# One accumulation instead of two for a sample's value tiles in a hybrid decoder step

## What is computed

```python
# group A, 8 heads of 64: forgetting attention over 1024 paged past tokens (8 pages of 128) and the own one
s = q @ kc * SCALE + (c_q - c_k)           # c: running sum of log-forget values
oa = softmax(s) @ vc
# group B, 8 heads of 64: the last 128 keys at strides 1, 4 and 16 and the own one,
# mixed by their softmax denominators
idx = pos - dil[None, :, None] * j         # dil = 1, 4, 16; j = 0..128
ob = sum_over_dil(w * softmax(q @ k[idx]) @ v[idx])
out = concat(oa, ob) @ w_out
```

## Time and profile before

| | |
|---|---|
| median of 3 runs | 2758.29 us (2755.62 to 2760.85) |
| profiled execution, own time | 2759.74 us |
| its span in the profile | 2757.9 us, 43275 instructions |
| mean granted TensorE clock | 0.979 of full speed |
| busy: PE, PEld | 2631.2 us (95%), 2402.2 us (87%) |
| busy: DVE, ACT, POOL | 1161.8 (42%), 543.9 (20%), 1121.1 us (41%) |
| values of samples L1102 | 192 matmul instructions |
| gathers L1083 | 128 matmul instructions |
| sums L1068 | 128 matmul instructions |
| masks L1291 | 16, median 744 ns |

### The profile page before, as it was taken

The page is one execution under the profiler, slowest core; times in us unless marked ns, Lnnn a source line. Parts: engine busy times, 40 slices in busy tenths (PEclk is TensorE's granted clock), DMA queues, the critical chain, the costliest instruction groups (busy, mean ns, idle before and its releaser), DMA issues.

```text
span 2757.9 us, 43275 instructions
## 1 busy us (share of the span) xinstructions
PE 2631.2 (95%) x16553; PEld 2402.2 (87%) x16553; DVE 1161.8 (42%) x2274; ACT 543.9 (20%) x1263; POOL 1121.1 (41%) x726
## 2 busy tenths in 40 slices
PE   5899988989999999999999998998999999999999
PEld 3787765556689999999999996898999999999999
DVE  4763735656615433333333343144453333333333
ACT  3210106555622100000000033312210000000001
POOL 4423214454575444444443345414464444333330
PEclk8999999999999999999999999999999999999999
DMA  4222226656620211111111111111021111111101
GB/s 116 60 76 85 76 64 190 191 185 193 186 79 16 70 47 46 46 46 46 49 49 46 46 38 35 43 32 47 16 62 47 47 49 49 46 46 49 50 31 62
DMA packets 220766, 189.88 MB, mean 69 GB/s; under 512 B 29571, under 2 KB 173443, under 8 KB 220644
## 3 DMA queue, kind: packets, MB, share of 16 engines
q1 hardware_dynamic: 202084, 163.99, 20.4%
q10 hardware_dynamic: 18560, 24.25, 2.5%
HBM read 171.19 MB, written 17.01 MB: 68 GB/s over the span
## 4 chain that ended last, share of the span: by engine, by line
PE 64%; DVE 4%; POOL 1%; ACT 1%; issue 1%; ACTq 0%; POOLq 0%; DVEq 0%
PE ps L489 61%; DVE hs L448 1%; PE ps L521 1%; PE ps L523 1%; PE ps L522 1%; POOL acc_sq L416 1%; ACT ps L1806 1%; DVE Xl L1881 0%; POOL Xl L462 0%; DVE Xl L462 0%; DVE acc_sq L440 0%; PE ps L1781 0%; POOL Wl L378 0%; PE ps L1918 0%; DVE VM_EARLY L1871 0%
## 5 line engine op out<-in xcount | busy, mean ns | idle before, releaser
L489 PE MATMUL ps<-Xh,Wh 128*128 128x256 f32 (+2 forms) x2712 | 875.6, 323 | 15.3 <-DVE Xl L1881 6.5
L489 PE MATMUL ps<-Xl,Wh 128*128 128x256 f32 (+2 forms) x2712 | 869.6, 321 | 0.0
L489 PE MATMUL ps<-Xh,Wl 128*128 128x256 f32 (+2 forms) x2712 | 868.5, 320 | 0.0
L364 POOL TENSOR_TENSOR Wh<-raw,zeros 128x1024 fp32r<-128x1024 f32 x185 | 367.1, 1984 | 1136.0 <-PE ps L489 790.0
L489 PEld LDWEIGHTS ps<-Xh,Wh 128*128 128x128 f32 x2712 | 512.4, 189 | 20.6 <-issue 8.6
L489 PEld LDWEIGHTS ps<-Xl,Wh 128*128 128x128 f32 x2712 | 512.5, 189 | 1.0 <-issue 0.3
L489 PEld LDWEIGHTS ps<-Xh,Wl 128*128 128x128 f32 x2712 | 512.8, 189 | 0.0
L367 POOL TENSOR_TENSOR Wl<-raw,Wh 128x1024 fp32r<-128x1024 f32 x185 | 455.9, 2464 | 14.5
L1597 DVE TENSOR_TENSOR Hl<-hf,Hh 128x392 fp32r<-128x392 f32 (+1 forms) x132 | 181.3, 1373 | 464.7 <-ACT Hh L1525 464.7
L489 PE MATMUL ps<-Hh,Wh 128*128 128x392 f32 (+2 forms) x1056 | 341.5, 323 | 2.4 <-DVE xT L1606 2.3
L489 PE MATMUL ps<-Hl,Wh 128*128 128x392 f32 (+2 forms) x1056 | 338.7, 321 | 0.0
(11 more groups left out here) (201 smaller groups left out, 2530.3 us busy)
## 6 DMA issues: line engine op xcount, KB each, us to landing
raw<-in_w_gate_up SPq DMA_DIRECT2D x88, 512.0 KB, 3.8
raw<-in_w_down SPq DMA_DIRECT2D x44, 512.0 KB, 3.5
kring<-in_cache_a_k SPq DMA_DIRECT2D x64, 256.0 KB, 3.7
ring<-in_cache_a_v SPq DMA_DIRECT2D x64, 256.0 KB, 3.3
raw<-in_w_in_even SPq DMA_DIRECT2D x25, 512.0 KB, 4.2
raw<-in_w_in_c SPq DMA_DIRECT2D x16, 512.0 KB, 3.8
xs<-in_x_prompt SPq DMA_DIRECT2D x8, 512.0 KB, 4.6
q_prompt<-zt ACTq DMA_DIRECT2D x16, 256.0 KB, 2.0
```

The lines of the kernel that those rows point to most:

```text
L364: pool.tensor_tensor(h[:, :], r[:, :], zeros[:, :].to_broadcast([P, 1024]), ALU.add).then_inc(split_high, 1)
L489: ins = nc.tensor.matmul(out, w, x, start=(j == 0), stop=(j == len(pairs) - 1))
```

## The change

The twelve tiles are accumulated in one step at distance 8 (`VALUES_AT`), three groups of four side by side, semaphore `values_ps`. Page heads keep columns 0 to 7 of `Lp`, the dilated heads get columns 8 to 15, so that the exponential is two instructions and bank 7 holds 16 used rows in each 32. The step waits for all eleven ring slots. The sums need one product for each row group instead of two, there is one reciprocal column and one mask over 128 rows, and one gather of four products with two columns of `hmask` that keep page and dilated rows apart. The copy to `oS` is one instruction. The order and the turns in which the sync engine issues the loads stay; only the name of the semaphore changes.

```diff
-        TURN_AT, SPREAD_AT, SUM_AT, PAGES_AT, DILATED_AT = 6, 7, 8, 8, 9
+        TURN_AT, SPREAD_AT, SUM_AT, VALUES_AT = 6, 7, 8, 8
...
-                    positive_wait(sp, page_ps if j < PAGES else dil_ps, it)
+                    positive_wait(sp, values_ps, it)
...
-                    for g in range(2):
-                        for i in range(4):
-                            last = nc.tensor.matmul(ps[i * LW:(i + 1) * LW, 6, 3 * P + g:3 * P + g + 1], Ls[:, g, :], ones[:, 0:1],
-                                                    start=True, stop=True)
-                if sample_at(u, PAGES_AT + 2) is not None:
-
-                    pe.wait_ge(dch, DCH * sample_at(u, PAGES_AT + 2) + 10)
-                    last = gather(sample_at(u, PAGES_AT + 2), 0)
-                if sample_at(u, DILATED_AT + 2) is not None:
-                    pe.wait_ge(osamp, 2 * sample_at(u, DILATED_AT + 2) + 1)
-                    last = gather(sample_at(u, DILATED_AT + 2), 1)
+                    for i in range(4):
+                        last = nc.tensor.matmul(ps[i * LW:(i + 1) * LW, 6, 3 * P:3 * P + 1], Ls[:, :], ones[:, 0:1], start=True, stop=True)
+                if sample_at(u, VALUES_AT + 2) is not None:
+                    last = gather(sample_at(u, VALUES_AT + 2))
...
-                pe.wait_ge(dmask, 2 * it + g + 1)
+                pe.wait_ge(dmask, it + 1)
                 for c in range(4):
-                    last = nc.tensor.matmul(ps[:, 6, 3 * P + 8 + c:3 * P + 9 + c], MV[0:MROWS[g], c * P:(c + 1) * P],
-                                            ones[0:MROWS[g], 0:1],
-                                            start=True, stop=True)
+                    last = nc.tensor.matmul(ps[:, 6, 3 * P + 2 * c:3 * P + 2 * c + 2], MV[:, c * P:(c + 1) * P],
+                                            hmask[:, HEADS:HEADS + 2], start=True, stop=True)
...
                 pe.wait_ge(dp_done, it + 1)
-                for j in tiles:
-                    if ring_slot(j) is not None:
-                        pe.wait_ge(ring_in[ring_slot(j)], 16 * (it + 1))
+                for j in VALUE_ORDER:
+                    pe.wait_ge(ring_in[ring_slot(j)], 16 * (it + 1))
...
-                for n, j in enumerate(tiles):
-                    rows = slice(LW * (n % 4), LW * (n % 4) + LW)
-                    last = nc.tensor.matmul(ps[rows, 7, :], Lp[:, j, :], value_tile(j), start=(n < 4), stop=(n + 4 >= len(tiles)))
-                last.then_inc(done, 1)
+                for j in range(LOG):
+                    rows = slice(LW * (j % 4), LW * (j % 4) + LW)
+                    last = nc.tensor.matmul(ps[rows, 7, :], Lp[:, j, :], value_tile(j), start=(j < 4), stop=(j + 4 >= LOG))
+                last.then_inc(values_ps, 1)
...
-                    act.activation(Lp[:, :, 0:HEADS], Lb[:, :, :], ACT.Exp).then_inc(dp_done, 1)
+                    act.activation(Lp[:, 0:PAGES + 1, 0:HEADS], Lb[:, 0:PAGES + 1, :], ACT.Exp)
+                    act.activation(Lp[:, PAGES + 1:LOG, HEADS:2 * HEADS], Lb[:, PAGES + 1:LOG, :], ACT.Exp).then_inc(dp_done, 1)
...
-                if sample_at(u - 1, PAGES_AT) is not None:
-                    sample_mask(sample_at(u - 1, PAGES_AT), 0, u + 1)
-                if sample_at(u - 1, DILATED_AT) is not None:
-                    sample_mask(sample_at(u - 1, DILATED_AT), 1, u + 1)
+                if sample_at(u - 1, VALUES_AT) is not None:
+                    sample_mask(sample_at(u - 1, VALUES_AT), u + 1)
```

## The result

The changed kernel takes 2780.6 us (median of 5 runs, 2773.5 to 2781.5), the kernel before in the same comparison 2760.9. The ratio is 1.0068, 95% interval 1.005 to 1.0085: slower by 18.8 us by the ratio (the two medians are 19.8 apart). The forecast was 10 us slower, with 2777 as the upper end of its range; the sign was right, the size came out nearly double, above that end. The profiled execution took 2780.6 us, its span is 2778.8.

A forecast was written before the change was run, and what follows sets the result against it. TensorE's fixed instruction order was taken to bound the attention stage (busy 44.4 of 50 us). Savings -21.2, late-tile waits +21.1 and clock +10.4 gave +10.3 us: forecast 2768 us, 8-in-10 range 2752 to 2777.

The forecast's parts named there:

- (a): TensorE's values: joint step takes 2.70 us like the page step, the dilated step goes, saving 7.9 us.
- (b): Masks: the second mask and TensorE's waits for it go, saving 5.4 us; three page-mask waits stay.
- The late last tile: Joint step waits for the last dilated tile, issued late by the sync engine: 21.1 us added, bounds 12 and 26.
- The clock: TensorE's granted clock falls to half after the new long waits: 10.4 us added, bounds 0 and 13.5.
- the two short ones: Idle stretches of 2.5 and 2.4 us at the joint step, counted at three quarters of a 2.3 us clock loss.
- the savings: Dilated step, masks, gathers, sums and end of stage together: 21.2 us saved, bounds 17 and 23.
- only two gathers be swallowed at the borders: Of eight saved gathers, the first and fourth samples' lie within other waits; six count, 6.4 us.
- (c, e): Gathers saved, 6.4 us, the last one 1.87; VectorE's last dilated mask ahead of the final reciprocal, 0.7 us.

The follow-up runs named there:

- step_late: Changed kernel with the joint step one unit later (distance 9), loads in their old turns: 2739.2 us, ratio 0.9923 against the kernel before.
- wait_only: Kernel before, with only the page step's wait extended to all eleven ring tiles: 2789.4 us, ratio 1.0094.
- load_early: Changed kernel with the last value tile issued one turn earlier by the sync engine: 2762.1 us, ratio 1.0001 against the kernel before.
- wait_each: Changed kernel at distance 8, each ring tile waited for right ahead of its own product: 2760.6 us, ratio 0.9995 against the kernel before.
- fill_wait: Changed kernel with TensorE multiplying the identity by itself ahead of its ring wait: 2765.6 us, ratio 1.002 against the kernel before.
- split_only: Kernel before, with GpSimd's second early weight split one turn earlier: 2760.1 us, ratio 0.9992.
- each_early_split: Changed kernel at distance 8, a wait for each tile, last value tile and GpSimd's second early weight split one turn earlier: 2748.7 us, ratio 0.9954 against the kernel before.

## Why the forecast was right in sign and half in size

1. **The joint step costs what the page step did (a).** Right: where the clock was full, for sample 3, it runs from 581.22 to 583.94, 2.72 us; `step_late` shows that the savings arrive.
2. **The masks (b).** Right: 5.4 us forecast, 5.4 found, with the three page waits left (2.1).
3. **The late last tile.** Right in place and size: forecast 6.9, 6.1, 2.9, 2.5, 2.4 and 0.3 us in samples 5, 6, 7, 1, 2 and 3, +21.1 in all; measured, over the waits already there, 6.2, 6.6, 2.9, 2.9, 1.7 and 0.2, +20.5 in six waits. `wait_only` shows that this wait alone makes a slower kernel, `load_early` and `wait_each` that taking it away gives the loss back.
4. **The clock.** Right in kind, a size too small: forecast 10.4, measured 13.3 by `fill_wait`, at the edge of its bounds. The term was sized from four borders, after waits of 2.1 to 4.6 us. After the long ones the half clock covered the whole joint step as well (5.1 us in place of 2.7). And one more fell where I had no wait in the list, at unit 55:

```profile
758.62 0.44 PE L1039 MATMUL ps<-ident,rl 128*64 128x128 f32 x4 [1.63 <-DVE rl L1221]
...
759.21 1.54 PE L1075 MATMUL ps<-hmask,MV 128*128 128x2 f32 x8
760.62 1.95 PE L1027 MATMUL ps<-ident,S 128*128 128x128 f32 x8
```

Of the six ring waits five were followed by half clock, all but the one of 0.2 us, where I had taken the two short ones at three quarters. "After none of the waits of up to 1.57 us did it" was the picture of one execution and not a bound: in `split_only`, the same program up to unit 62, the mask waits of 0.93 and 1.24 us around the first sample were each followed by some 3 us at half clock, and in the kernel before they were not; the last gather in the earlier trace rows ran at half clock behind waits of 0.81 and 0.95; and of the five versions with the step at distance 8, four have half clock behind the 1.63 us at unit 55 and `fill_wait` has not.

   The Trainium skill, "TensorE: Matmul & The Clock Gate", Part 1, has throttled as the default which activity lifts. That by it every wait counts in full was the forecast's inference; the rule of thumb in the page's section on HAM oscillation warns of long idle gaps only, and nothing in it makes the short ones count. The traces decide: short ones counted in most executions and not in all.

5. **The step that failed: the savings, put at 21.2 us with 17 as their least.** The time says 15.0: 20.5 of waits and 13.3 of clock, less the 18.8 measured. The profiled stage says 12.0 (20.5 + 13.9 - 22.4). The sum let only two gathers be swallowed at the borders, on the premise that a border's wait shrinks or grows only by what TensorE does ahead of it, and that the transfer behind it lands as before. The waits for the reciprocals rose by 7.0 us in the profile, and in three ways. (That they would not shrink to give the added lateness back held.)

   At unit 55 (above) the removed dilated step (0.99 and a mask wait of 0.40) came back as a wait of 1.63 for the reciprocal. All five profiles at distance 8 have this wait, at 1.62 or 1.63, and none of the others. The fifth border's wait grew by 0.6. These 2.2 us are saved work that another engine took back.

   At the second border the wait grew by 2.3. There VectorE waits for a bias transfer that ScalarE issues at a fixed place of its queue; VectorE's part, before and then in the changed kernel, and under each the time from issue to landing of that transfer:

```profile
507.53 0.75 DVE L1225 CUSTOM_DVE_ANT_0 S<-ps,bias,mx_tail 128x512 f32<-128x512 f32 x1 [2.57 <-DMA bias<-c_dram]
...
DMA to landing us min/median/max: 4.8/4.8/4.8
```

```profile
510.95 0.75 DVE L1213 CUSTOM_DVE_ANT_0 S<-ps,bias,mx_tail 128x512 f32<-128x512 f32 x1 [4.14 <-DMA bias<-c_dram]
...
DMA to landing us min/median/max: 6.2/6.2/6.2
```

   0.9 of the 2.3 is the gather, as the forecast had it. The other 1.4 is the transfer itself, 6.2 us to landing in place of 4.8. At the fourth border the wait for a transfer of the position table (`dist`) went from 0.98 to 3.01 and TensorE's from 2.13 to 3.81, and TensorE arrives there as long after the issue as before (3.34 us): all of the 1.7 is the transfer and what follows it, which landed after 5.1 us in place of 3.8. The forecast held these landings fixed without a reason. In the five profiles at distance 8 the second border's transfer takes 5.3 to 6.2 us and the fourth's 4.5 to 5.9, in the six others 4.6 to 5.8 and 3.4 to 5.6. While the second one was on its way, the DMA engines were busy 0.93 of the time in the changed kernel and 0.74 before. That the change makes them land later by bringing other loads closer would fit; no run tests it, and `split_only` had 8.0 us at the third border with no change there. So these 3.1 us stay open between the change and chance.

   `step_late`, which takes the work out one unit away, has 16.6 us of these waits; `each_early_split`, at distance 8, 19.2. That it is the place, and not something else that goes with it, is only partly shown: see the open part there.

6. **The end of the stage (c, e).** Forecast 1.87 and 0.7 us saved; nothing came. I followed the chain to VectorE's last gather, but from O of unit 62 the order on GpSimd sets the end: the two parts of unit 62 (L963, L965), the split of the weight tile (L364, L367), the two parts of unit 63. The timeline of the changed kernel:

```profile
797.00 0.29 DVE L1228 TENSOR_TENSOR O<-ps,Rs 128x128 f32<-128x128 f32 x1 [2.01 <-issue]
...
800.23 2.34 POOL L367 TENSOR_TENSOR Wl<-raw,Wh 128x1024 fp32r<-128x1024 f32 x1
800.23 2.41 DVE L1327 TENSOR_TENSOR Xl<-oS,Xh 128x64 fp32r<-128x64 f32 x1
802.52 0.40 POOL L963 TENSOR_TENSOR Xh<-O,zeros 128x128 fp32r<-128x128 f32 x1
...
803.00 0.46 POOL L965 TENSOR_TENSOR Xl<-O,Xh 128x128 fp32r<-128x128 f32 x1
...
803.56 0.67 PE L489 MATMUL ps<-Xh,Wh 128*128 128x392 f32 x1 [4.91 <-DVE Xl L1327]
```

From 797.00 to 803.56 is 6.56 us, to the hundredth what it was before. `split_only` moved it to 4.36. The 2.6 us that I had counted there are part of the error.

By time the forecast fell 8.5 us short (18.8 against 10.3): the waits came out 0.6 smaller, the clock 2.9 larger, the savings 6.2 smaller. Of the savings, points 5 and 6 name 2.2, 3.1 and 2.6 us in the profile, where 9.2 are missing. The range ended at 2777 because its lower bound for the savings, 17, left room for one more mask wait and two more gathers, and for nothing at unit 55, at the end of the stage or in the transfers. That the sign came out right rests on the late tile and the clock, both shown by experiments of their own.

## What to carry to other kernels

When two steps with different inputs are merged, the merged one is due when its last input lands: read the issue and landing of each input against the start of the earlier step, before counting what the merge saves, and put the step or the wait (one for each tile) there. A wait on TensorE can have a second price in its clock, so work moved into it can be free or better. One profile shows one execution: before a wait of a few us is read as an effect, look how far it moves between executions of the same program. And a saving counts only up to the next point that a transfer or another engine fixes.

## What the runs showed of the hardware beside this

VectorE's subtraction of 64 columns with both inputs in SBUF took 2.41 us beside GpSimd's pass of 2.34 us, both from 800.23 on; before, it began 0.08 us after that pass had ended:

```profile
777.83 2.34 POOL L367 TENSOR_TENSOR Wl<-raw,Wh 128x1024 fp32r<-128x1024 f32 x1
...
780.25 0.35 DVE L1343 TENSOR_TENSOR Xl<-oS,Xh 128x64 fp32r<-128x64 f32 x1
```

There it took 0.35, though GpSimd's next, short pass (780.13, 0.40 us) lay across it. In `step_late` it began 0.22 us after the long pass and ended 0.08 after it (759.08 and 2.24 us, against 758.86 and 2.38), so it lasts until GpSimd is done, and not a fixed time. The Trainium skill, "SBUF — State Buffer", SBUF: two separate sides, has VectorE and GpSimd share a port pair that one of them locks for a whole instruction, which such an operation with two SBUF inputs needs against a GpSimd operation that reads SBUF; the traces agree, with 2.41 and 2.24 against 0.35 us.

The runs of the changed kernel fall in two groups, 2773.5 to 2774.0 and 2780.6 to 2781.5, with a mean granted clock of 0.976 to 0.977 in the first and 0.971 to 0.974 in the second. It fits halved clocks that some runs escape; no run here tests it.
